# Seven weight slots instead of six in the expert stage of a hybrid decoder step, with the sample rows first and the output projection in column halves

## What is computed

```python
x = x + g1 * (concat([o_nsa, o_dn]) @ w_out)          # g1: one row for the prompt, one for each sample sequence
h = rmsnorm(x, norm_ffn_g) * (1 + sc2) + sh2
lg = h @ router_group_w + router_group_b              # 4 groups, best one taken
le = (h @ router_expert_w + router_expert_b)          # 8 experts in it, best two taken
for e in range(32):
    he = silu(h @ w_gate[e]) * (h @ w_up[e])          # 1024 -> 256
    y = y + gates[:, e:e+1] * (he @ w_down[e])        # 256 -> 1024
x = x + g2 * y;  out = rmsnorm(x, final_norm_g)
```

## Time and profile before

| | us |
|---|---|
| median of three runs | 1028.65 |
| the profiled execution | 1032.61 |
| its span | 1030.7 |
| start of the stage (first projection matmul) | 631.02 |
| last projection matmul ends | 699.3 |
| first expert product | 737.99 |

### The profile page before, as it was taken

The page is one execution under the profiler, slowest core; times in us unless marked ns, Lnnn a source line. Parts: engine busy times, 40 slices in busy tenths (PEclk is TensorE's granted clock), DMA queues, the critical chain, the costliest instruction groups (busy, mean ns, idle before and its releaser), DMA issues. The chain is left out here.

```text
span 1030.7 us, 21027 instructions
## 1 busy us (share of the span) xinstructions
PE 953.2 (92%) x8032; PEld 615.2 (60%) x8032; DVE 438.6 (43%) x937; ACT 315.3 (31%) x713; POOL 281.8 (27%) x403
## 2 busy tenths in 40 slices
PE   6899999999799999899899999999899999999795
PEld 5456777777566766787455665455455555555441
DVE  2131000002658345577678762446522333333237
ACT  5100000000646423244577542111022232333244
POOL 7000000033100337920456432000223343434213
PEclk9899999999999999999999999999899998899898
DMA  9975742713650038000744254928699999999972
GB/s 311 353 270 201 261 163 82 163 53 113 221 187 7 1 42 178 20 4 8 190 121 125 70 198 160 302 97 320 225 363 381 386 396 375 385 376 376 370 281 102
DMA packets 90506, 212.16 MB, mean 206 GB/s; under 512 B 31730, under 2 KB 54954, under 8 KB 76510
## 3 DMA queue, kind: packets, MB, share of 16 engines
q1 hardware_dynamic: 77666, 187.36, 53.3%
q0 software_dynamic: 9984, 20.15, 6.0%
q10 hardware_dynamic: 2756, 3.27, 0.9%
HBM read 254.83 MB, written 33.95 MB: 280 GB/s over the span
## 5 line engine op out<-in xcount | busy, mean ns | idle before, releaser
L592 PE MATMUL PS<-hT,wring 128*128 128x288 f32 x256 | 83.6, 408 | 0.0
L2492 POOL DMA_INDIRECT ys_dram<-late,ids x47 | 43.4, 924 | 146.2 <-ACT late L2728 120.1
L593 PE MATMUL PS<-hT,wring 128*128 128x288 f32 x256 | 83.0, 406 | 0.0
L2927 DVE COPY mixT<-PS 128x128 f32<-128x128 f32 x49 | 14.3, 292 | 159.9 <-PE PS L2607 159.9
L2486 POOL DMA_INDIRECT mixT<-h_dram,ids x49 | 47.3, 966 | 105.6 <-DVE ids L2894 87.6
L2588 PE MATMUL PS<-ring,mixT 128*64 128x256 f32 x304 | 71.9, 391 | 2.2 <-DVE mixT L2913 2.2
L2589 PE MATMUL PS<-ring,mixT 128*64 128x256 f32 x304 | 71.9, 391 | 0.0
L2588 PEld LDWEIGHTS PS<-ring,mixT 128*64 128x64 f32 x304 | 42.7, 142 | 31.9 <-issue 10.9
L592 PEld LDWEIGHTS PS<-hT,wring 128*128 128x128 f32 x256 | 48.2, 190 | 17.2 <-DVE xc L203 2.6
L593 PEld LDWEIGHTS PS<-hT,wring 128*128 128x128 f32 x256 | 48.6, 190 | 13.4
L2520 PE MATMUL PS<-late,mixT 128*128 128x512 f32 x128 | 55.5, 593 | 0.9 <-PEq L3013 0.9
(11 more groups left out here) (591 smaller groups left out, 2172.7 us busy)
## 6 DMA issues: line engine op xcount, KB each, us to landing
ring<-in_expert_w_gate_dram SPq DMA_DIRECT2D x27, 1024.0 KB
ring<-in_expert_w_up_dram SPq DMA_DIRECT2D x27, 1024.0 KB
ring<-in_expert_w_down_dram SPq DMA_DIRECT2D x27, 1024.0 KB
late<-in_w_ada_dram SPq DMA_DIRECT2D x8, 2048.0 KB
mod_r<-in_expert_w_gate_dram SPq DMA_DIRECT2D x9, 1024.0 KB
mod_r<-in_expert_w_up_dram SPq DMA_DIRECT2D x9, 1024.0 KB
mod_r<-in_expert_w_down_dram SPq DMA_DIRECT2D x9, 1024.0 KB
late<-in_expert_w_gate_dram SPq DMA_DIRECT2D x7, 1024.0 KB
```

The source lines that it names most:

```text
L592: MM(PS[:, b, 0:HALF], lhs, hT[:, k, 0:HALF], **s)
L593: last = MM(PS[:, b + 1, 0:HALF], lhs, hT[:, k, HALF:NTOK], **s)
L2492: pool.indirect_dma_start(m.ys_dram.ap(), bass.IndirectOffsetOnAxis(ap=ids[:, 1, j:j + 1], axis=0), yr(n), None, bounds_check=LAST_ROW, oo ...
```

## The change

- **Seven slots.** `RING = 7`. The new slot is `m.xa[:, 0:SLOT]`: the buffers `x2` and `aux` become one, `xa`, and the slot covers the residual rows and the first half of `aux`. The residual rows are therefore written to a buffer in memory, `x2_dram` (2.36 million bytes), and read back at the end. Place 4 takes this slot, and is loaded last, when the second gather has landed. `mod_r` and `h2x` are slots 5 and 6. The overflow tiles are attached to places 7, 9, ... 27 and 8, 12, ... 28.
- **Projection by column halves.** `w_out` lies in `late` as two halves; each prompt tile is projected over the first half of its columns, then, after all tiles, over the second. The sample tile is first, both halves at once. The order of tiles (`LINE`) is sample, 0, 1, 2, 3. Place 3's gate and up weights are loaded once the first halves are over.
- **Rows turned two tiles ahead.** `turn(n+2)` and `take_x(n+2)` in place of `n+1`, with three buffers `xT`.
- `rows`, `mod_f`, `fg` and `diag` move to other buffers, and `diag` is made after the last tile's copies.

```diff
-RING = 6
+RING = 7
-NPAIR = 12
-ATTACH = [RING + 2 * o for o in range(NPAIR)] + [RING + 3 + 4 * k for k in range(NOV - NPAIR)]
+NPAIR = 11
+ATTACH = [RING + 2 * o for o in range(NPAIR)] + [RING + 1 + 4 * k for k in range(NOV - NPAIR)]
...
+        LINE = [PT] + list(range(PT))
+        STEPS = [(PT, 0)] + [(i, half) for half in range(2) for i in range(PT)]
+        whole = lambda i: 1 if i == PT else TILES + 1 + i
-        slots = [m.ring[:, x] for x in range(3)] + [m.late[:, 0:SLOT], modr[:, :], m.h2x[:, :]]
+        slots = [m.ring[:, x] for x in range(3)] + [m.late[:, 0:SLOT], m.xa[:, 0:SLOT], modr[:, :], m.h2x[:, :]]
...
+            def keep_x2(i):
+                sp.wait_ge(x2_ok, whole(i))
+                sp.dma_start(m.x2_dram.ap()[i * P:i * P + ROWS[i], :], m.x2[0:ROWS[i], i, :]).then_inc(x2_out, 16)
+
+            keep_x2(PT)
             sp.wait_ge(y_ps, TILES)
-            load_base(3)
+            load_gate_up(3)
+            for i in range(PT - 1):
+                keep_x2(i)
+            sp.wait_ge(y_ps, len(STEPS))
+            load_down(3)
+            keep_x2(PT - 1)
             sp.wait_ge(h_ok, TILES)
-            load_base(4)
+            load_base(5)
             sp.wait_ge(hT_ps, TILES)
             sp.wait_ge(h_out, 16 * TILES)
-            load_base(5)
+            load_base(6)
+            sp.wait_ge(x2_out, 16 * TILES)
+            sp.wait_ge(r_in[1], 16)
+            load_base(4)
...
+            for i in range(TILES):
+                sp.dma_start(m.x2[0:ROWS[i], i, :], m.x2_dram.ap()[i * P:i * P + ROWS[i], :]).then_inc(x_in[i], 16)
...
-            for i in range(TILES):
-                y(i)
-                if i >= 2:
-                    logits(i - 2)
-                if i:
-                    turn_rows(i - 1)
+            for s in range(len(STEPS)):
+                y(s)
+                if s == 2:
+                    turn_rows(0)
+                elif s == 3:
+                    logits(0)
+                elif s >= TILES + 1:
+                    if s >= TILES + 2:
...
-                if n + 1 < NT:
-                    turn(n + 1)
+                if n == 0:
+                    turn(1)
+                if n + 2 < NT:
+                    turn(n + 2)
...
+            def residual(s):
+                i, half = STEPS[s]
...
                 else:
+                    dve.wait_ge(mods_in, 16 * NB)
...
             dve.wait_ge(mod_in, 16)
-            for i in range(TILES):
-                dve.wait_ge(x_in[i], 16)
-                if i == PT:
-                    dve.wait_ge(mods_in, 16 * NB)
-                residual(i)
-                if i:
-                    turned(i - 1)
-                modulated(i)
-                if i >= 2:
-                    take_logits(i - 2)
+            for s in range(len(STEPS)):
+                residual(s)
+                if s == 1:
+                    modulated(0)
+                elif s == 2:
+                    turned(0)
...
+                dve.wait_ge(x_in[i], 32)
```

More of the change, by code:

```diff
@@ L2329, in stage_moe @@
         moved = end[:, 3 * D:5 * D].rearrange("p (s n) -> p s n", s=2)
-        rows = [a[:, 0:TILES * D].rearrange("p (i n) -> p i n", n=D) for a in (m.late[:, 0:SLOT], modr[:, :])]
+        rows = [a[:, 0:TILES * D].rearrange("p (i n) -> p i n", n=D) for a in (m.h2x, m.ring[:, 0])]
         rwe, rwg = h2[:, PT, 0:KD * NE], h2[:, PT, KD * NE:KD * (NE + NG)]
@@ L2509, in _, with y @@
             MM = nc.tensor.matmul
-            def y(i):
-                r, b = ROWS[i], 2 * (i % 2)
-                if i >= 2:
-                    pe.wait_ge(x2_ok, i - 1)
+            def y(s):
+                i, half = STEPS[s]
+                if s >= 4:
+                    pe.wait_ge(x2_ok, s - 3)
                 if i < PT:
+                    for c in range(8):
+                        last = MM(PS[:, s % 4, :], m.mixT[:, c, i * P:(i + 1) * P], wo[:, half, c, :], start=(c == 0), stop=(c == 7))
+                else:
                     for half in range(2):
-                        if i == 0:
-                            pe.wait_ge(m.wo_in[half], 16)
-                        for c in range(8):
-                            last = MM(PS[0:r, b + half, :], m.mixT[:, c, i * P:i * P + r], wo[:, c, half * HALF:(half + 1) * HALF], start=(c == 0), stop=(c == 7))
-                else:
+                        pe.wait_ge(m.wo_in[half], 16)
                     for c in range(8):
                         for half, side in enumerate((R, Q)):
-                            last = MM(PS[side, b, :], m.mixT[:, c, i * P:i * P + r], wo[:, c, half * HALF:(half + 1) * HALF], start=(c == 0), stop=(c == 7))
+                            last = MM(PS[side, s % 4, :], m.mixT[:, c, i * P:i * P + ROWS[i]], wo[:, half, c, :], start=(c == 0), stop=(c == 7))
                 last.then_inc(y_ps, 1)
             def turn_rows(j):
-                r = ROWS[j]
+                i = LINE[j]
+                r = ROWS[i]
                 pe.wait_ge(h_ok, j + 1)
@@ L2743, in _ @@
                     take_down(n)
-                if n == RING:
-                    act.wait_ge(own_ok, 1)
-                    for c in range(TOPK):
-                        last = nc.scalar.activation(diag[:, c, :], m.ident[:, :], ACT.Copy, scale=share[:, c, 0:1])
-                    last.then_inc(diag_ok, 1)
             take_down(NT - 1)
+            act.wait_ge(own_ok, 1)
+            for c in range(TOPK):
+                last = nc.scalar.activation(diag[:, c, :], m.ident[:, :], ACT.Copy, scale=share[:, c, 0:1])
+            last.then_inc(diag_ok, 1)
             def shared(i):
@@ L2960, in _ @@
                     take_hidden(n - 1)
-                if n + 1 < NT:
-                    take_x(n + 1)
-                hidden(n)
+                if n == 0:
+                    take_x(1)
+                    hidden(0)
+                if n + 2 < NT:
+                    take_x(n + 2)
+                if n:
+                    hidden(n)
                 if n == EARLY:
```

101 lines of the change are left out of this document (60 added, 41 removed).

## The result

The changed kernel takes 1048.03 us (median of 4 runs, 1038.15 to 1053.12) where the kernel before took 1031.24 beside it (4 runs): the ratio is 1.0155, 95% interval 1.0097 to 1.0214. So it is slower by 16 to 19 us; forecast were 9, with a range up to 1046. The profiled execution spans 1051.6 us, 20.9 more than that of before.

A forecast was written before the change was run, and what follows sets the result against it. Two nearly level chains, the weight stream and TensorE's expert tiles, were taken to bound it. Stream's end +8.0 (+14.6 - 9.35 + 2.8) and residual rows +1 made +9 on 1028.65: 1037.6 us, range 1024 to 1046.

The forecast's parts named there:

- Sample tile first: Projection: TensorE's first turn stalls 13.0 us for the sample tile's late gates; projection's end +14.6 us in sum.
- The term of 2.4 us: Projection: +2.4 us added to the 13.0 us stall in the sum for the projection's end.
- Halves, writes, router: Projection by column halves, writing residual rows to memory, router and lists: 0 us each; last-step difference bounded -1 to +1.
- Two tiles ahead: Expert loop: products no longer wait for the copy of their rows, -3.0 us on TensorE, bounds 0 and -8.
- The seventh slot: Weight stream: 14.6 us later start, 9.35 less for one expert prefetched, 2.8 for place 4's late load: end +8.0 us.
- Its 2 us to start: Place 4's load behind the second gather: about 2 us to start, within the 2.8 us by which it is too long.
- Residual rows: Tail: reading them back delays the experts' rows by 1 us beyond the stream's 8, bounds 0 and 5.8.
- TensorE's chain: Loop's end: place 28 waits 1 us, fuller clock -2.4, one copy wait less -0.5; last scatter there at about 996.2.
- the rows in full: Rival, tail: residual reads cost all 5.8 us and the clock stays low longer; +17.7 us, 1046 us; chance 0.15.

The follow-up runs named there:

- e11: Changed kernel with the first turn after the projection's fifth step and its logits after the sixth, gates in their old place; ratio 1.0040 to the kernel before.
- e12: The changed kernel itself, unaltered, measured again on another chip; ratio 1.0185 to the kernel before.
- e2: Changed kernel with the sample tile's rows and gates issued first and the first turn two steps later; ratio 0.9998 to the kernel before.
- e13: e2 with six slots, overflow tiles attached as before, residual rows left in place and diagonal blocks written early; ratio 0.9971 to the kernel before.
- e3: Changed kernel with the fifth slot's gate and up weights requested without waiting for the gathered rows; ratio 1.0152 to the kernel before.
- e16: e2 with diagonal blocks written early and residual rows neither written to memory nor read back, seven slots kept; ratio 0.9974 to the kernel before.
- e10: e2 with diagonal blocks written early and residual rows written to memory but not read back; ratio 0.9974 to the kernel before.
- e7: e2 with the tenth overflow tile tied to place 10 and not to place 27; ratio 1.0048 to the kernel before.
- e17: Changed kernel with the first turn two steps later and each tile's residual rows read back behind that tile's experts' rows; ratio 1.0013 to the kernel before.
- e18: The kernel of e11 measured again, on one chip with e17; ratio 1.0033 to the kernel before.
- e14: e2 with diagonal blocks written early and each tile's residual rows read back behind that tile's experts' rows; ratio 0.9969 to the kernel before.

## Why the prediction was wrong

- **Sample tile first, +14.6: right.** Gates at 656.5 (forecast 656), turn at 665.3 (664.9), stall 12.4 (13.0), projection's end at 714.6 (712 to 716), first expert product at 752.9 (751 to 754). The term of 2.4 us is 6.10 less 3.67 from the earlier trace rows, behind the wait of 4.7 us; here the nine matmuls behind the stall took 2.3 us more than at the rate ahead of it (6.2 for 3.9). e11 against e12 gives the price in the run times: 0.0145.
- **Halves, writes, router, 0: right.** e2, e11 and e13 have the projection at 67.8 us, before 68.3, and no wait of over 1 us in it.
- **Two tiles ahead, -3.0:** neither shown nor refuted.
- **The seventh slot, +8.0 on the stream: the size was about right** (place 28's weights at 975.1 for 965.7, the last ones +11.1). Its 2 us to start had no row; in the trace of before, 128 transfers of 64 KB, in five groups, took 1.8 to 2.1 us from issue to landing (medians). In TensorE's chain it had less weight than I gave it: e3 moved the stream's end by 11 us and the time by nothing that four runs show, and e16 and e13 have the same time with and without the slot. TensorE had 235 us of products in a loop of 250.5.
- **Residual rows, +1: this is the step that failed.** I let the reads pay 4.5 us behind the last weights, at 410 GB/s, for which I had no row, and had them hidden but for 1. I had counted when the output gates and `fg` are issued, but not that their transfers stand between the weights and the reads. Before, these landed 4.6 us behind the last weights (992.8 and 988.2); in the changed kernel 6.1 us behind (1005.4), and the residual rows another 6.4 us later, at 1011.8: 12.5 us and not 4.5. In the nine other profiles with the reads ahead it is 11.6 us or more. In the tail this shows as a scatter 2.2 us longer (7.71 for 5.50) and first rows 3.3 us longer (8.0 for 4.7 from their request), together close to the term's upper bound of 5.8; 2.5 us more lie between the first rows' landing and the end (37.3 for 34.8). e10, without the reads (the gates' place and the blocks differ too), is 7 us faster than e11.
- **TensorE's chain, -2.9 for the last scatter: this failed beside it.** I had the scatter landed at 996.2; it landed at 1006.2. Up to place 28 the chain ran as forecast (975.1 for 973.7, 0.9 of it the stage's later start). From there to the scatter's start it took 23.4 us, in e12 again, where 19.8 were taken before and I forecast 16.9. The clock was one part: place 28 waited 3.6 us, not 1, and its products ran low (0.55), 6.6 us for the 16 that took 3.67 in the earlier trace rows. The order of the last tiles was the other, and I hadn't looked at it. Before, an empty overflow tile stood between places 27 and 28, and place 27's down products were over when TensorE waited for place 28. Now an empty tile stands between 28 and 29 instead, and the chain holds place 27's down products too (982.46), then place 28's (985.12), then a wait for place 29's hidden rows (991.92):

```profile
982.46 0.64 PE PS L2644
...
985.12 0.64 PE PS L2644
...
991.92 0.61 DVE mixT L2958
...
993.41 0.57 PE PS L2644
```

Before, only those of places 28 and 29, one behind the other:

```profile
977.73 0.64 PE PS L2624
...
980.39 0.64 PE PS L2624
```

- **Both paths were late by some 10 us**: the last scatter landed at 1006.2 for 996.2, and the residual rows were back at 1011.8, where I had the experts' rows start behind them at 1001.3. So mending one alone needn't give the time back: e7 mended the order and its tail grew, e17 moved the reads and gained some 2 us.
- **The rival that came near.** The condition that I had written down for the rows in full, "if the weights' last DMA lands after SP has issued the residual rows, which I expect", held (999.3 against 992.3), and I still gave that case 0.15. Its time, 1046, is 2 us below one median and level with the other (1045.83). That is in part luck: 3.9 of its 17.7 us were a slower clock and VectorE work in the projection, which lasted as forecast, and it had nothing for the order of the tiles.
- What I hadn't in the sum at all: transfers under way in SP's queue slow the scatter that others wait for, though the scatter is in another queue. It took 7.1 us in e18, with the residual rows and the output gates beside it, 5.3 in e17 with the output gates, and 2.0 in e14, where these had landed. The DMA share alone doesn't tell it: 0.86, 0.35 and 0.44. By what way the transfers hold the scatter up, no run shows.

The 2.5 us behind the first rows have no experiment of their own, and over the 20 profiles this stretch varies from 33.5 to 39.5 us. Two things in the changed kernel's profile can hold them. TensorE had waited 5.8 us for the rows, and its first four products then took 3.75 us (granted clock 0.50 from 1014.4 to 1018.2), the next four 1.72:

```profile
1019.40 1.72 PE PS L2717 x4
```

And two of VectorE's last sums, one for each tile, were longer than the 1.22 us of the others:

```profile
1022.80 3.22 DVE L3020 TENSOR_TENSOR xa<-xa,mod_r 128x1024 f32<-128x1024 f32 x1
...
1027.19 1.22 DVE L3020 TENSOR_TENSOR xa<-xa,mod_r 128x1024 f32<-128x1024 f32 x1
...
1030.98 2.15 DVE L3020 TENSOR_TENSOR xa<-xa,mod_r 128x1024 f32<-128x1024 f32 x1
```

Before, these sums all took 1.22 or 1.23 us, but one scaling took 3.18, so only part of this is new.

## What to carry to other kernels

When a change puts work first in its stage, date its operands, not only the place that it leaves: eight small transfers that nobody needed for 60 us became a 12 us stall, and an instruction order two steps later took it away (projection 67.8 us for 82.7). Reads that an end needs late belong behind the reads that it needs first (some 2 us here, hardly clear of the noise). Before counting on free room in a stretch, list what already stands in the queue ahead of the new transfers: the output gates and `fg` did here. And where two chains run level, take away one of them in thought before paying for it: an earlier stream, an earlier last scatter and a seventh slot each brought nothing alone that the runs could tell, and the profiles show the other chain taking over.

## What the runs showed of the hardware

- In the changed kernel's tail VectorE's instructions without a PSUM operand got longer beside GpSimd's additions (2.35 us each, at 1022.60, 1029.69 and 1033.14): the sum at 1022.80 took 3.22 us and the one at 1030.98 2.15, others 1.22; the scaling at 1033.24 took 3.33 and others 1.28. The product at 1029.73, which reads PSUM, stayed at 1.22. So the two that began within 0.2 us of an addition became 2.0 and 2.1 us longer, and the one that began 1.06 us before an addition's end 0.9 us.
- The time goes with TensorE's mean granted clock. Of the kernel before, runs with 0.963 to 0.965 took 1043 to 1049 us, runs with 0.983 to 0.985 1023 to 1031: about 0.8 us for 0.001. Between kernels that differ by 3 us that is much of the scatter, and I know no edit here that moved it.
- While the eight transfers of the sample's gates were under way (644 to 656) the DMA share was 1.03 at 195 GB/s; with weights, gathers and scatters the same share moves 379 (752.9 to 980), with weights 406 (656 to 676). The share is the mean of all 16 engines, so all were busy in the slow stretch, and not some of them only, as I had read it.
- The chips differ in more than the clock: in the loop TensorE's waits for VectorE's copies of hidden rows were 2.7 us on the chip of e11 and 8.0 on that of e2, with the copies themselves at 0.29 us on both. Over all profiles they are 2.4 to 2.9 us on three chips and 5.2 to 10.2 on the three others, whatever the kernel; no run shows why.
